# Residual product of a hybrid diffusion backbone cut into four 64x64 blocks, with half of each residual row stored in the other partitions

## Chip, core and metric

The kernel is one program on one core of one Trainium2 chip. The metric is the device time of one launch in microseconds (us); smaller is better. TensorE (PE) multiplies, VectorE (DVE), ScalarE (ACT) and GpSimd (POOL) work elementwise, SyncE (SP) issues most of the loads and stores. PSUM is the memory into which TensorE writes; a bank of it is 512 f32 columns wide on 128 partitions.

## Reference

The reference runs two layers over 1024 latent tokens of 1024 channels. Layer 0 has windowed attention beside a gated linear attention, layer 1 a short gated convolution. Both layers end with a mixture of experts, whose result is added to the residual stream and normalised:

```python
y = hier_moe(tokens, router_wg[l], ..., moe_w1[l], moe_w3[l], moe_w2[l])   # top group, then top-2 of 8 experts
h_lat = post_norm(h_lat, m[5] * y[:B * S].reshape(B, S, D), ln_w[l, 1], ln_b[l, 1])
# post_norm(x, y, w, b) = layer_norm(DEEPNORM_ALPHA * x + y, w, b),  DEEPNORM_ALPHA = (2 * DEPTH) ** 0.25
```

The change concerns the term `DEEPNORM_ALPHA * x` of this last line, in both layers. Everything is f32.

## The kernel before, in words

The 1024 tokens are eight tiles t = 0 to 7 of 128 rows. Each engine has its own instruction stream, written out in order; semaphores tie the streams together.

In `moe(l)` the experts' rows are computed in 21 steps. POOL scatters the rows of a step, already weighted by the gate, to the DRAM tensor `y_rows` (two rows for each token). SP loads the experts' weights piece by piece into slots. When the last piece of a slot has been used, SP fills four of these slots (`ROW_SLOTS`) with the residual rows `h_rows` of two tiles each, and after the last scatter it loads the pairs of expert rows, `pair[t]`, one load for each tile (two half loads for tile 0).

Then comes the stage of this document, the combination. For each tile TensorE makes the sum alpha * x + y in a pair of PSUM banks, (4, 5) for even tiles and (0, 1) for odd ones:

- `residual_part(l, t)` multiplies the residual row tile `row_at[t]` by `alpha_i`, alpha times the identity, once for each 512 columns. It waits for the slot's load and, for t >= 2, for `nrm` of tile t - 2, which frees the banks.
- `combined(l, t)` adds the two expert rows of each token: the tokens 0 to 63 of the tile from `pair[t][:, 0]` and 64 to 127 from `pair[t][:, 1]`, each by a stationary matrix of 128x64, so that two products go to the two halves of the partitions.

TensorE runs the residual products of tiles 0 and 1 right behind `moe(l)`, then `combined` for each tile (with the residual product inside it for t >= 2). In layer 0 the transposes `stream_T(t - 1)` (line 818) follow each `combined`, for the convolution of layer 1; behind the last tile come the products of the convolution (line 1367). Two products `gate_rows` (line 886) stand between the first tiles.

DVE takes the statistics of the sum (1990, 1998), ACT the root (1609), DVE the reciprocal and the offset (2003, 2005), ACT writes the normalised tile (1613) and so sets `nrm`. In layer 1 POOL multiplies the tile by the weight (2661) and DVE adds the bias (2304), two tiles later in its order; SP stores the output. In layer 0 DVE and ACT also copy the transposed tile (1742, 1481), and POOL makes sums of tiles 4 to 6 for the convolution (2636 to 2643), DVE those of tile 7 (2370 to 2377).

Each f32 product is two records in the trace. A semaphore of a slot counts 16 for each load; `filled` works out the count to wait for from `FILLS` and `ROW_LOADS`.

Of the kernel before, what the change touches and what calls it, by code (L numbers as in the profile page):

```python
# [13 lines left out]
P = 128  # L14
# [38 lines left out]
SLOTS = 19  # L53
# [6 lines left out]
SLOT_OF, BEFORE, LAST_IN, FILLS, _held = {}, {}, {}, [0] * SLOTS, []  # L60
# [7 lines left out]
    LAST_IN[_slot] = _piece  # L68
    _held = sorted(_held + [(freed(_piece), _n, _slot, _piece)])
ROW_SLOTS = (9, 11, 14, 15)  # L70
ROW_LOADS = [int(n <= 8 or n in ROW_SLOTS) for n in range(SLOTS)]


def filled(slot, l, turn):

    return 16 * ((FILLS[slot] + ROW_LOADS[slot]) * l + turn + 1)

# [77 lines left out]
def program(nc, T, out):  # L155
# [5 lines left out]
    with ctx:  # L161
        sems = {}

        def S(name):

            if name not in sems:
                sems[name] = ctx.enter_context(nc.semaphore(name))
            return sems[name]

        def sb(name, shape, dt=f32):  # L170
            return ctx.enter_context(nc.sbuf_tensor(name, shape, dt))
# [30 lines left out]
        alpha_i = sb("alpha_i", [P, P])  # L202
# [7 lines left out]
        def bank(b, n=1):  # L210
            return banks[b // 2][:, (b % 2) * 512:(b % 2 + n) * 512]
# [54 lines left out]
        h_dram = [nc.dram_tensor(f"h_rows{l}", [SEQ, D], f32, kind="Internal").ap() for l in range(DEPTH)]  # L266
# [80 lines left out]
        row_at = [blocks[:, 12 + t, :] for t in range(4)] + [hh[:, t] for t in range(4, NT)]  # L347
# [157 lines left out]
        for _s in range(len(SETS)):  # L505
            conv_order += [(_s, n) for n in ((1, 2) if _s >= 2 else ()) + (6, 5, 7, 3, 4)]
        copy_order = [(s, n) for s, (_, m) in enumerate(SETS) for n in ((1, 2, 5) if m == 2 else (1, 2, 5, 4))]
        sum_order = [(s, n) for s, (_, m) in enumerate(SETS) for n in ((11, 22, 12, 21) if m == 2 else (11, 22, 12))]

        def conv_loaded(s):  # L510
# [30 lines left out]
        def _(sp):  # L541
            def load(dst, src, name, **how):
                sp.dma_start(dst, src, **how).then_inc(S(name), 16)  # L543
# [78 lines left out]
            for n, (t0, t1) in enumerate(WOUT_A):  # L622
                sp.wait_ge(S("g_o"), max(t0, t1) + 1)
                for g in range(2):
                    rows = slice(HD * g, HD * g + HD)
# [75 lines left out]
            for l in range(DEPTH):  # L701
# [35 lines left out]
                def last_use(slot):  # L737
                    m, h, q = LAST_IN[slot]
                    if m < 2:
                        sp.wait_ge(S(f"h_mm{l}"), 4 * LAST[q] + 2 * m + h + 1)  # L740
                    else:
                        sp.wait_ge(S(f"y_mm{l}"), LAST[q] + 1)
# [3 lines left out]
                for n, slot in enumerate(ROW_SLOTS):  # L746
                    last_use(slot)
                    dst = blocks[:, 12 + 2 * n:14 + 2 * n, :] if n < 2 else hh[:, 2 * n:2 * n + 2]
                    load(dst, h_dram[l][2 * n * P:2 * (n + 1) * P, :].rearrange("(t p) n -> p t n", p=P), f"w_in_{slot}")
                sp.wait_ge(S("routed"), 8 * l + 8)  # L750
                n_over = sp.value_load(ov[0:1, OVER + 1:OVER + 2], min_val=0, max_val=OVER)
                with sp.If(0 < n_over):
# [25 lines left out]
                for t in range(NT):  # L778
                    rows = y_dram[l][t * 2 * P:(t + 1) * 2 * P, :].rearrange("(h p) n -> p h n", h=2)
# [32 lines left out]
        def _(pe):  # L812
            mm, tp = nc.tensor.matmul, nc.tensor.transpose
# [14 lines left out]
            for k in range(KC):  # L828
                if k % 2 == 0:
                    pe.wait_ge(S(f"ada_in{k // 2}"), 16)  # L830
                for n in range(4):
                    last = mm(bank(0)[32 * n:32 * n + 32, :], cond[:, k, :], ada_first[:, k, n * 512:(n + 1) * 512],
                              start=(k == 0), stop=(k == KC - 1))
# [3 lines left out]
            for k in range(KC):  # L837
                for h in range(2):
                    last = mm(bank(1)[64 * h:64 * h + 64, 4 * k:4 * k + 4], cols(mrow)[:, k, :], cc("pick")[:, 4 * h:4 * h + 4],
                              start=True, stop=True)  # L840
# [562 lines left out]
            def sum_at(t):  # L1403
                return (4, 0)[t % 2]

            def residual_part(l, t):

                slot = ROW_SLOTS[t // 2]
                pe.wait_ge(S(f"w_in_{slot}"), filled(slot, l, FILLS[slot]))
                if t >= 2:  # L1410
                    pe.wait_ge(S("nrm"), NT * (2 * l + 1) + t - 1)
                for n in range(2):
                    mm(bank(sum_at(t) + n), alpha_i[:, :], row_at[t][:, n * 512:(n + 1) * 512], start=True, stop=False,  # L1413
                       skip_group_check=True)

            def combined(l, t):

                if t == 0:
                    pe.wait_ge(S("share_ok"), l + 1)
                if t >= 2:  # L1420
                    residual_part(l, t)
                pe.wait_ge(S(f"w_in_{t}"), filled(t, l, FILLS[t]))
                for n in range(2):
                    if t == 0 and n:
                        pe.wait_ge(S("w_in_8"), filled(8, l, FILLS[8]))
                    for h in range(2):
                        last = mm(bank(sum_at(t) + n)[64 * h:64 * h + 64, :], share[:, t, h, :],  # L1427
                                  pair[t][:, h, n * 512:(n + 1) * 512], start=False, stop=True, skip_group_check=True)
                last.then_inc(S("comb"), 1)
# [13 lines left out]
            for t in range(2):  # L1443
                residual_part(0, t)
# [21 lines left out]
            for t in range(2):  # L1466
                residual_part(1, t)
# [1219 lines left out]
```

## Time and profile before

| | us |
|---|---|
| median of 3 runs | 2289.83 |
| lowest, highest | 2288.42, 2290.57 |
| the profiled execution: its own time | 2290.16 |
| the profiled execution: first to last instruction (span) | 2288.3 |
| TensorE busy | 2166.8 |
| VectorE busy | 808.2 |
| ScalarE busy | 402.3 |
| GpSimd busy | 350.7 |
| mean granted TensorE clock, share of full speed | 0.984 |

The time of the profiled execution is the span and 1.9 us around it. The busy times overlap, and they are sums over the whole program; what a stage of a few microseconds costs is read from the rows of that stage.

### The profile page before, as it was taken

The page shows a single profiled execution, that of the slowest core. Times are in us where ns is not written, and L with a number is a line of the kernel's source. Part 1 is how long each engine was busy: PE and PEld are TensorE (multiplying, and loading weights), DVE is VectorE, ACT ScalarE, POOL GpSimd, SP SyncE. Part 2 cuts the span into 40 slices and gives each one's busy share as a digit, 9 for nine tenths or more (in the row PEclk, how much of TensorE's full clock was granted, in tenths as well). Part 3 has the DMA queues.
Part 4 walks back from the last instruction along what each step waited for, and adds up shares of the span by engine and source line. Part 5 has one row for each costly group of instructions (what it writes and reads, how often), then busy time and mean ns, then how long its engine had stood idle before and what let it go on. Part 6 is the DMA issues. An engine that isn't in the chain of part 4 may idle for free. (4 is left out here: it accounts for less than half of the span.)

```text
span 2288.3 us, 27969 instructions
## 1 busy us (share of the span) xinstructions
PE 2166.8 (95%) x10576; PEld 1047.0 (46%) x10576; DVE 808.2 (35%) x1711; ACT 402.3 (18%) x862; POOL 350.7 (15%) x382
## 2 busy tenths in 40 slices
PE   6999999999999999999997999999998999999996
PEld 3547545777554343434432444444553343334431
DVE  2694213656626311111111633334455111111114
ACT  2301042554211110111110500000111111010112
POOL 0000012222131101100100413221320010201003
PEclk8999999999999999999999999999999999999998
DMA  9892000001436999999998411114337999999997
GB/s 388 332 372 81 1 0 1 2 2 39 145 97 246 371 419 419 419 414 419 409 419 350 175 41 52 37 55 165 141 113 279 417 419 419 408 420 419 411 396 296
DMA packets 135816, 572.50 MB, mean 250 GB/s; under 512 B 25049, under 2 KB 38521, under 8 KB 93690
## 3 DMA queue, kind: packets, MB, share of 16 engines
q1 hardware_dynamic: 123002, 537.04, 59.2%
q0 software_dynamic: 12672, 33.57, 3.8%
q8 instruction: 89, 1.46, 0.3%
q14 instruction: 53, 0.43, 0.1%
HBM read 548.52 MB, written 34.62 MB: 255 GB/s over the span
## 5 line engine op out<-in xcount | busy, mean ns | idle before, releaser
L1291 PE MATMUL bank<-bigA,bigB 128*32 128x512 f32 (+2 forms) x1888 | 478.4, 598 | 13.6 <-DMA bigA<-in_moe_w 8.3
L867 PE MATMUL bank<-bigC,bigB 128*128 128x512 f32 (+3 forms) x768 | 293.7, 538 | 0.0
L1291 PEld LDWEIGHTS bank<-bigA,bigB 128*32 128x32 f32 (+2 forms) x1888 | 157.6, 133 | 237.5 <-issue 229.5
L1315 PE MATMUL bank<-bigA,bigB 128*32 128x512 f32 (+2 forms) x912 | 242.5, 594 | 6.3 <-DVE bigB L2241 3.1
L867 PEld LDWEIGHTS bank<-bigC,bigB 128*128 128x128 f32 x768 | 143.4, 194 | 128.4 <-issue 119.8
L1291 PE MATMUL bank<-bigC,bigB 128*32 128x512 f32 (+2 forms) x560 | 171.4, 593 | 0.0
L1367 PE MATMUL bank<-bigB,bigA 128*128 128x512 f32 x384 | 170.7, 592 | 0.0
L1481 ACT ACTIVATE bigB<-bank,small 128x128 f32<-128x128 f32 x280 | 104.3, 459 | 367.1 <-PE bank L818 367.0
L2565 POOL DMA_INDIRECT y_rows<-bigB,ints x42 | 42.3, 1007 | 810.5 <-DVE bigB L2246 810.5
L2246 DVE TENSOR_TENSOR bigB<-bank,gate 128x512 f32<-128x512 f32 x84 | 54.1, 686 | 236.5 <-PE bank L1315 236.5
L2237 DVE TENSOR_TENSOR bigB<-bigB,bank 128x512 f32<-128x512 f32 x42 | 28.9, 688 | 303.8 <-PE bank L1291 303.8
L1315 PEld LDWEIGHTS bank<-bigA,bigB 128*32 128x32 f32 (+2 forms) x912 | 80.3, 135 | 107.0 <-issue 101.9
L1367 PEld LDWEIGHTS bank<-bigB,bigA 128*128 128x128 f32 x384 | 72.8, 190 | 90.9 <-issue 90.9
L1626 ACT ACTIVATE bigB<-bank 128x512 f32<-128x512 f32 x42 | 25.1, 597 | 498.4 <-PE bank L1291 498.4
L1163 PE MATMUL bank<-bigB,bigA 128*128 128x512 f32 x256 | 112.7, 594 | 0.0
L1367 PE MATMUL bank<-bigA 128*128 128x512 f32 x240 | 109.0, 593 | 2.3 <-issue 1.2
L2241 DVE COPY bigB<-bank 128x256 f32<-128x256 f32 x42 | 17.8, 424 | 243.0 <-PE bank L1299 243.0
L1291 PE MATMUL bank<-misc,bigB 128*32 128x512 f32 (+2 forms) x320 | 101.8, 594 | 1.9 <-DMA bigA<-in_moe_w 1.4
L1315 PE MATMUL bank<-bigC,bigB 128*32 128x512 f32 (+2 forms) x400 | 100.8, 594 | 1.8 <-DMA bigA<-in_moe_w 1.8
L1784 DVE SCALAR_TENSOR_TENSOR lnwb<-bigA,misc,lnwb 128x1024 f32<-128x1024 f32 x70 | 89.9, 1284 | 5.1 <-DMA bigA<-in_ada_w 0.8
L1742 DVE TENSOR_SCALAR bigB<-bank,small 128x128 f32<-128x128 f32 x216 | 73.8, 403 | 25.6 <-PE bank L818 23.2
L1291 PEld LDWEIGHTS bank<-bigC,bigB 128*32 128x32 f32 (+2 forms) x560 | 52.4, 128 | 56.1 <-issue 55.4
(351 smaller groups left out, 2597.0 us busy)
## 6 DMA issues: line engine op xcount, KB each, us to landing
bigA<-in_moe_w SPq DMA_DIRECT2D x250, 1024.0 KB, 24.9
bigC<-in_moe_w SPq DMA_DIRECT2D x80, 1024.0 KB
bigA<-in_ada_w SPq DMA_DIRECT2D x40, 1024.0 KB, 6.8
misc<-in_moe_w SPq DMA_DIRECT2D x36, 1024.0 KB, 24.8
lnwb<-in_moe_w SPq DMA_DIRECT2D x18, 1024.0 KB, 25.9
bigA<-y_rows SPq DMA_DIRECT2D x14, 1024.0 KB, 10.7
bigA<-in_w_in_odd SPq DMA_DIRECT2D x12, 1024.0 KB, 5.2
bigA<-in_ada_w SPq DMA_DIRECT2D x4, 2048.0 KB, 13.6
```

Source lines behind the costliest of these rows:

```text
L867: last = mm(bank(n % 3)[:, 0:w], uT[:, k, t * P:(t + 1) * P], wring[:, g % 2, k, at_:at_ + w], start=(k == 0), stop=(k == KC - 1))
L1163: last = mm(bank(2 * ((t + 1) % 2) + n), zT[:, t, k, :], wout1[:, k, n * 512:(n + 1) * 512], start=(k == 0), stop=(k == KC - 1))
L1291: last = mm(bank(m)[at_:at_ + w, :], xT[:, j, KC // 2 * h + k, at_:at_ + w], w13_at(SLOT_OF[m, h, q][0], k), start=(h == 0 and k == 0), st ...
L1315: last = mm(bank(6 + n)[at_:at_ + w, :], gT[:, 2 * h + k, at_:at_ + w], w2_at(SLOT_OF[2, h, q][0], k)[:, n * 512:(n + 1) * 512], start=(h ...
L1367: last = mm(bank(b[s % 2]), lhs[:, k, :], rhs(k), start=(first and k == 0), stop=(k == 3), skip_group_check=True)
L1481: last = go(dst[k], bank(b + k // 4)[:, (k % 4) * P:(k % 4 + 1) * P], ACT.Identity, bias=shift[:, k:k + 1], scale=scale[:, k:k + 1])
L1626: go(sg, bank(0), ACT.Silu).then_inc(S(f"silu_a{l}"), 1)
L1742: last = v.tensor_scalar(dst[k], bank(b + 1)[:, (k - 4) * P:(k - 3) * P], scale[:, k:k + 1], shift[:, k:k + 1], MUL, ADD)
L1784: V(v.scalar_tensor_tensor(acc[:, r % 2], part, cond[:, k, 0:1], acc[:, r % 2], MUL, ADD))
L2237: v.tensor_tensor(gg, sg, bank(1), MUL).then_inc(S(f"g_d{l}"), 1)
L2246: v.tensor_tensor(yo[:, j, n * 512:(n + 1) * 512], bank(6 + n), gate[:, 1, n * 512:(n + 1) * 512], MUL)\
L2565: pool.indirect_dma_start(out=y_dram[l], out_offset=bass.IndirectOffsetOnAxis(ap=rows, axis=0), in_=yo[:, j], in_offset=None, bounds_check ...
```

## The change

The residual product of a tile is two products of 128 rows by 128 columns before. Since `alpha_i` is diagonal, only two of the four 64x64 blocks of each hold anything. Now these blocks alone are multiplied: four products of 64 rows by 64 columns for each tile, one in each quarter of the array. For this the second 512 columns of each residual row lie in the other half of the partitions: rows 64 to 127 of the tile in partitions 0 to 63 and the other way round. In the products of the first 512 columns (n = 0) block u reads and writes half u; in those of the second (n = 1) it reads half u and writes the other half. The load of two tiles becomes three: one for the first columns, two for the second.

```diff
-ROW_LOADS = [int(n <= 8 or n in ROW_SLOTS) for n in range(SLOTS)]
+ROW_LOADS = [3 * (n in ROW_SLOTS) + (n <= 8) for n in range(SLOTS)]
...
-                    load(dst, h_dram[l][2 * n * P:2 * (n + 1) * P, :].rearrange("(t p) n -> p t n", p=P), f"w_in_{slot}")
+                    rows = h_dram[l][2 * n * P:2 * (n + 1) * P, :].rearrange("(t p) n -> p t n", p=P)
+                    load(dst[:, :, 0:512], rows[:, :, 0:512], f"w_in_{slot}")
+                    for u in range(2):
+                        load(dst[64 * u:64 * u + 64, :, 512:], rows[64 - 64 * u:128 - 64 * u, :, 512:], f"w_in_{slot}")
...
-                pe.wait_ge(S(f"w_in_{slot}"), filled(slot, l, FILLS[slot]))
+                pe.wait_ge(S(f"w_in_{slot}"), filled(slot, l, FILLS[slot] + ROW_LOADS[slot] - 1))
...
                 for n in range(2):
-                    mm(bank(sum_at(t) + n), alpha_i[:, :], row_at[t][:, n * 512:(n + 1) * 512], start=True, stop=False,
-                       skip_group_check=True)
+                    for u in range(2):
+                        rows, to = slice(64 * u, 64 * u + 64), 64 * (u ^ n)
+                        mm(bank(sum_at(t) + n)[to:to + 64, :], alpha_i[rows, 64 * u:64 * u + 64], row_at[t][rows, n * 512:(n + 1) * 512],
+                           start=True, stop=False, skip_group_check=True)
```

On TensorE, in the combination of layer 0, tiles 2 and 3 (818 the transposes of the tile before, 1413 the residual product, 1427 the product with the expert rows), the kernel before has:

```order
L818 MATMUL bank<-misc,bigC 128x128 x8
L1413 MATMUL bank<-bigA,alpha_i 128x512 x2
L1427 MATMUL bank<-bigA,bigB 64x512 x4
L818 MATMUL bank<-misc,bigC 128x128 x8
L1413 MATMUL bank<-bigA,alpha_i 128x512 x2
L1427 MATMUL bank<-bigA,bigB 64x512 x4
```

And the changed kernel, whose lines are numbered three to five higher:

```order
L821 MATMUL bank<-misc,bigC 128x128 x8
L1418 MATMUL bank<-bigA,alpha_i 64x512 x4
L1432 MATMUL bank<-bigA,bigB 64x512 x4
L821 MATMUL bank<-misc,bigC 128x128 x8
L1418 MATMUL bank<-bigA,alpha_i 64x512 x4
L1432 MATMUL bank<-bigA,bigB 64x512 x4
```

Nothing changes its place; two products of the residual become four smaller ones.

On SP, behind the last expert weights of a layer (`ln_w` and `ln_b` are the parameters of the norm, `h_rows` the residual rows), before:

```order
L543 DMA bigA<-in_moe_w 128x2x1024
L543 DMA lnwb<-in_ln_w 128x1024
L543 DMA lnwb<-in_ln_b 128x1024
L543 DMA bigA<-h_rows 128x2x1024 x2
L543 DMA bigC<-h_rows 128x2x1024 x2
```

And after:

```order
L543 DMA lnwb<-in_ln_w 128x1024
L543 DMA lnwb<-in_ln_b 128x1024
L543 DMA bigA<-h_rows 128x2x512
L543 DMA bigA<-h_rows 64x2x512 x2
L543 DMA bigA<-h_rows 128x2x512
L543 DMA bigA<-h_rows 64x2x512 x2
L543 DMA bigC<-h_rows 128x2x512
L543 DMA bigC<-h_rows 64x2x512 x2
L543 DMA bigC<-h_rows 128x2x512
L543 DMA bigC<-h_rows 64x2x512 x2
```

Four loads become twelve, of the same bytes, in runs of 2048 bytes where they were of 4096.

## Rows read from the trace of the kernel before

**Rows 1.** The page, its first line.

```profile
span 2288.3 us, 27969 instructions
```

**Rows 2.** Chain that ended last, layer 1, behind the last scatter: start us, us, what.

```profile
2235.80 7.66 DMA y_rows<-bigB,ints
2243.48 4.09 DMA bigA<-y_rows
```

**Rows 3.** Layer 0: timeline (start, us, operation [idle before]); last, a group (busy, mean ns).

```profile
1270.34 1.16 PE L818 MATMUL bank<-misc,bigC 128*128 128x128 f32 x8
1271.34 1.88 PE L1413 MATMUL bank<-bigA,alpha_i 128*128 128x512 f32 x4
1273.15 1.94 PE L1427 MATMUL bank<-bigA,bigB 128*64 128x512 f32 x8
1275.02 1.16 PE L818 MATMUL bank<-misc,bigC 128*128 128x128 f32 x8
...
1284.49 1.30 DVE L1990 BATCH_NORM_STATS2 small<-bank 128x6 f32<-128x512 f32 x2 [1.07 <-PE bank L1427]
...
L1413 PE MATMUL bank<-bigC,alpha_i 128*128 128x512 f32 x16 | 7.5, 593 | 0.0
```

**Rows 4.** Timeline of TensorE in the attention of layer 0.

```profile
438.93 2.05 PE L1065 MATMUL bank<-bigA,bigC 128*128 128x128 f32 x16
440.91 1.10 PE L1097 MATMUL bank<-bigB,bigC 64*64 64x128 f32 x32
441.94 0.77 PE L970 MATMUL bank<-misc,bigB 128*128 128x128 f32 x5
```

**Rows 5.** Timeline of SP and TensorE, start of the combination of layer 0.

```profile
1237.40 1.55 SPq L543 DMA_DIRECT2D bigC<-h_rows  x2
...
1255.43 7.88 SPq L543 DMA_DIRECT2D bigA<-y_rows  x9
```

**Rows 6.** Timeline of TensorE, the same place.

```profile
1259.64 1.08 PE L1427 MATMUL bank<-bigA,bigB 128*64 128x512 f32 x4 [0.59 <-DMA bigA<-y_rows]
```

**Rows 7.** Timeline of the combination of layer 1.

```profile
2255.07 2.34 POOL L2661 TENSOR_TENSOR bigC<-bigC,lnwb 128x1024 f32<-128x1024 f32 x1 [18.29 <-ACT bigC L1613]
...
2256.17 1.26 DVE L2005 SCALAR_TENSOR_TENSOR small<-small 128x1 f32<-128x1 f32 x1
...
2258.75 2.34 POOL L2661 TENSOR_TENSOR bigC<-bigC,lnwb 128x1024 f32<-128x1024 f32 x1 [1.33 <-ACT bigC L1613]
...
2258.94 1.30 DVE L1990 BATCH_NORM_STATS2 small<-bank 128x6 f32<-128x512 f32 x2 [1.51 <-PE bank L1427]
...
2261.11 0.16 DVE L2005 SCALAR_TENSOR_TENSOR small<-small 128x1 f32<-128x1 f32 x1
...
2262.72 1.30 DVE L1990 BATCH_NORM_STATS2 small<-bank 128x6 f32<-128x512 f32 x2 [0.31 <-PE bank L1427]
...
2264.54 1.94 PE L1427 MATMUL bank<-bigA,bigB 128*64 128x512 f32 x8
...
2266.43 1.96 PE L1413 MATMUL bank<-bigC,alpha_i 128*128 128x512 f32 x4
...
2268.32 1.94 PE L1427 MATMUL bank<-bigA,bigB 128*64 128x512 f32 x8
```

**Rows 8.** Timeline, layer 0, where the combination hands over to the convolution.

```profile
1300.90 1.26 POOL L2636 TENSOR_TENSOR bigA<-bigB 128x512 f32<-128x512 f32 x1 [0.24 <-POOL misc L2643]
...
1309.01 1.48 DVE L2377 TENSOR_TENSOR misc<-bigB,bigA 128x256 f32<-128x256 f32 x1
...
1310.60 3.70 PE L1367 MATMUL bank<-bigA 128*128 128x512 f32 x8 [1.10 <-DVEq L2379]
```

**Rows 9.** Stretches: us, then busy us (instructions) by engine, PEclk, DMA share, GB/s.

```profile
1258.00:1260.00 2.00, 1.41 (x5) 0.42 (x5) 0.00 (x0) 0.91 (x2) 0.00 (x0) 1.00 1.03 381
1261.00:1264.00 3.00, 3.00 (x10) 0.95 (x12) 1.60 (x4) 1.69 (x3) 0.00 (x0) 1.00 1.03 415
1255.00:1257.00 2.00, 2.00 (x5) 0.95 (x4) 0.00 (x0) 0.00 (x0) 0.00 (x0) 0.75 0.13 37
```

## Prediction

> **What bounds the kernel now.** The change touches one stage, the combination behind the experts, once in each layer. So I read no shares of the whole but three views of that stage. The page gives the span, 2288.3 us [rows 1]; the execution's own time was 2290.16, so 1.9 lie around it, and the median shown, 2289.83, is 0.3 below it.
>
> The chain of waits comes first. It shows how the stage begins: the last scatter takes 7.66 us and the first load of expert rows 4.09 [rows 2]. Nothing of TensorE is on the chain there. In layer 0 SP has issued the residual loads by 1238.95 and issues the expert rows at 1255.43 [rows 5]; the first product with expert rows starts at 1259.64, behind 0.59 us of waiting for its load, with the first two residual products in front of it [rows 6]. So the residual products of tiles 0 and 1 are hidden, in both layers, and those of tiles 2 to 7 are what the change can pay for.
>
> The timeline of one tile comes second. In layer 0 a tile takes 4.68 us of TensorE without a gap: 1.00 for the transposes, 1.81 for the residual product, 1.87 for the expert rows (starts at 1270.34, 1271.34, 1273.15 and 1275.02); DVE waits 1.07 us for it in each tile [rows 3]. TensorE is the bound. In layer 1 the tile is two products, 1.89 and 1.89 us (2264.54, 2266.43, 2268.32), 3.78 in all, and DVE waits only 0.31 [rows 7]: two engines are near each other, and a third matters, below.
>
> The third view is what follows. Behind layer 0 the convolution is long TensorE work, then router and experts of layer 1, all started by this chain; I take it that what is won at its start is kept. Behind layer 1 only the norm of the last tile and the stores follow.
>
> **The product itself.** The trace before has blocks of this very shape. In the attention 32 records of 64x64 blocks with 128 columns start at 440.91, and the next work at 441.94: 1.03 us [rows 4]. The eight full 128x128 records of the same width take 1.00 [rows 3]. So four blocks go in the time of one record. For 512 columns the four records of a residual product are busy 1.88 us, of which the last is 0.59 [rows 3]; the three starts before it are 0.43 apart. Four blocks of two records each are two such steps. The expert product, which changes the cut of the array at both ends as the new one will, costs 1.87 for four steps, so 0.15 beyond them. The new product is 2 x 0.43 + 0.15 = 1.01.
>
> The cut of the array now changes in layer 0 where it did not, between transposes and residual product. A record of 128 columns is a quarter of 0.43, 0.107. Sixteen of them between two such changes take 440.91 - 438.93 = 1.98 [rows 4], 0.27 more than their steps, so 0.13 a change; the eight transposes behind one change take 1.00, 0.14 more. I take 0.1, since part of it may already stand in the 0.15. So the tile of layer 0 saves 1.81 - 1.01 - 0.10 = 0.70, six tiles **4.2 us**. In layer 1 a cut changes there already: 1.89 - 0.86 = 1.03.
>
> One thing differs from those rows. There the upper and lower rows of the array write different banks; here both write the same bank, in different halves of its partitions. Each half of the partitions still gets two banks from two row halves, as in the attention, so I expect no conflict. This is my main uncertainty and a rival below.
>
> **What layer 0 keeps.** The new tile needs 3.98 us. DVE's own work is 4.68 - 1.07 = 3.61, so TensorE stays the bound. At the hand-over three things meet: the DVE sums of tile 7 end at 1310.49, the convolution goes on at 1310.60 after waiting 1.10 us for them, and POOL has started its tile 6 at 1300.90 right behind tile 5 [rows 8]. POOL works back to back, 5.7 us a tile, and starts early by less than TensorE does (its tile 4 waits for the fifth tile of the chain, four savings, 2.8). So POOL's last tile lies further into DVE's sums. There the two take turns (next part), and walking through the turns I get the DVE sums 4.0 us earlier, not 4.2. TensorE's 1.10 us of waiting covers the rest. Layer 0 gives **-4.0**; without any of this -4.2, with no cover at all -3.0.
>
> **What layer 1 keeps.** By TensorE alone a tile would fall to 1.03 + 1.89 = 2.92, by DVE to 3.78 - 0.31 = 3.47. But see POOL. DVE's offset instruction, 0.16 us at 2261.11, took 1.26 at 2256.17 and so ended at 2257.43; POOL's product ran from 2255.07 to 2257.41 [rows 7]. I read that DVE's two-input operation from SBUF waits until POOL's ends. Then there is a loop: POOL's product ends, DVE's offset, ACT's write, POOL's next product. It is in the rows: POOL starts at 2255.07 and again at 2258.75, 3.68 us [rows 7]. The tile can't fall below 3.68 while POOL multiplies in it. The page "GPSIMD Engine Reference" of the Trainium skill (1. Specifications) says the same, that GpSimd's SBUF interfaces are shared with VectorE and contended by instructions with two SBUF inputs.
>
> Step by step: the statistics of tile 2 come 0.86 earlier than 2258.94. The offset would then run at 2260.25, while POOL's product (2258.75 + 2.34) ends at 2261.09; it ends at 2261.11, not at 2261.27: 0.16 won of 0.86. Each of the five tiles behind wins 3.78 - 3.68 = 0.10. Layer 1 gives 0.16 + 0.5 = **-0.7**. If POOL were no obstacle, 0.86 and then 0.31 a tile would give -2.4, cut to about -2.2 by tile 3, whose banks are not free before; that is the lower bound, 0 the upper.
>
> **What the loads cost.** Eight more issues take SP 0.5 to 0.8 us each (two took 1.55), some 5 us, up to about 1244; SP's next work is at 1255.43 [rows 5], so this is hidden, and uncovered it would be 5 us. The transfers are another matter. Runs of 2048 bytes (the first expert loads, 1258 to 1260) moved 381 GB/s, those of 4096 (1261 to 1264) 415 [rows 9], 9% more. The residual rows are 4.2 MB, 10.1 us at 415 and 11.0 at 381; eight more completions add little. Some queues still had residual rows when the expert loads were issued: the DMA share is 0.13 from 1255 to 1257 [rows 9], two engines of 16. These lag by up to 0.9 us more, and the first expert load needs all sixteen. Against that, the last scatter alternates with shorter packets and may end sooner. Bounds for each layer -0.5 and +1.0; I take +0.4 in layer 0, where the tail reached into the expert load, and **+0.5** for both.
>
> **Sum.** -4.0 - 0.7 + 0.5 = -4.2 us. The span goes to 2284.1, that execution to 2286.0, the median to 2285.6.
>
> **The rivals.**
>
> *A shared bank is a conflict.* The two blocks of a bank then run one behind the other, and a block of one bank beside a block of the other. The product has four steps, as before, and the change of cut costs 0.1 a tile in layer 0: +0.6, and +0.5 of loads, so +1.1, 2290.9. Against it: the two blocks write different partitions. For it: in [rows 4] the row halves write different banks, and no product before does otherwise. The page "TensorEngine Tiling (Array Packing)" of the Trainium skill (Restrictions and Gotchas, Gotcha 1) says that different row tiles can't access one PSUM bank at the same time, which would be this case. Chance 0.10.
>
> *The blocks run one behind the other altogether (slower).* Place: the residual product of tiles 2 to 7. Four blocks of two steps are 8 x 0.43 + 0.15 = 3.6 us instead of 1.81: +1.8 a tile, over 12 tiles +21; with three of four apart, 6 steps, +0.9 a tile and +11. Say 2300 to 2311. It decides from 4.5 steps on. For it only that no row shows one bank; against it [rows 4]. Chance 0.05.
>
> *POOL is no obstacle in layer 1.* The 1.26 us row is a single one, and DVE might have waited for something else. Then layer 1 gives -2.2 and the sum is -5.7: 2284.1. Chance 0.15.
>
> *The expert loads come later.* If the tail of the residual rows delays each first expert load by 1.0 to 1.5 us, the sum is -4.7 + 2.5 = -2.2: 2287.6. For it the tail [rows 9], against it that in layer 1 there are 7.66 us of scatter in which it drains [rows 2]. Chance 0.15. The opposite, scatters that end sooner by 0.5 a layer, gives -5.7 as well, chance 0.10.
>
> *The forecast*, -3.2 to -5.2: chance 0.45.
>
> **How the numbers follow.** 2285.6 is the forecast's. The range leaves out the serial cases and the best corner: 2283.2 to 2290.2. A measurement tells from no change about 0.2%, 4.6 us, that is 2285.2, close to the forecast; so the forecast's chance is split, 0.16 of it faster. With POOL or the scatter in its favour 0.25 more: faster 0.41. Slower by over 0.2% only with serial blocks or a cause I haven't seen: 0.09. The same: 0.50.
>
> **What would show it.** The four blocks' records should start together, and the residual product should take 1.0 us in place of 1.81, both layers. Layer 0: a tile of 4.0 us; DVE idle before the statistics about 0.4. Layer 1: POOL's products 3.7 us apart, DVE's offset ending with POOL's product in tile after tile, and TensorE waiting in each tile, for the norm or at the end, for the first time. The first product with expert rows, from the issue of its load, 4.1 us as before or up to a microsecond more. The stretch from there to the convolution's 1310.60 should be 4.0 shorter. I am wrong if the blocks of one bank start apart, if DVE's offset stays at 0.16 us while POOL multiplies, or if a later stage (the expert weights of layer 1 come at the pace of DMA) doesn't start earlier with TensorE.

## The result and the profile after

The changed kernel takes 2297.59 us (median of 6 runs, 2294.34 to 2299.26), the kernel before 2289.76 in the runs beside it (6 runs, 2288.42 to 2290.59). The ratio is 1.0033, 95% interval 1.0023 to 1.0044: slower by 0.3%. The forecast was 2285.6 with a range to 2290.2. The profiled execution has a span of 2295.6 us, 7.3 more than [rows 1].

The product did what was forecast. The timeline of TensorE in layer 0 (start, us, operation, idle before it), for [rows 3]:

```profile
1264.01 1.08 PE L1432 MATMUL bank<-bigA,bigB 128*64 128x512 f32 x4 [2.15 <-DMA bigA<-y_rows]
...
1270.05 1.16 PE L821 MATMUL bank<-misc,bigC 128*128 128x128 f32 x8
1271.14 1.09 PE L1418 MATMUL bank<-bigA,alpha_i 64*64 64x512 f32 x8
1272.16 1.94 PE L1432 MATMUL bank<-bigA,bigB 128*64 128x512 f32 x8
...
1276.14 1.94 PE L1432 MATMUL bank<-bigA,bigB 128*64 128x512 f32 x8
```

The residual product takes 1.02 us (1271.14 to 1272.16) for 1.81, and a tile 3.98 (1272.16 to 1276.14) for 4.68. But the first expert product starts at 1264.01, not 1259.64 as in [rows 6], after waiting 2.15 us for its load. In layer 0 the gain is used up before the stage has begun. SP's timeline, for [rows 5]: twelve issues of rows for four, and the expert rows are issued at 1257.57 for 1255.43.

```profile
1235.77 4.74 SPq L543 DMA_DIRECT2D bigA<-h_rows  x6
1240.55 7.14 SPq L543 DMA_DIRECT2D bigC<-h_rows  x6
1257.57 7.28 SPq L543 DMA_DIRECT2D bigA<-y_rows  x8
```

The chain of waits in layer 1, for [rows 2], shows where the time goes: the last scatter takes 10.96 us for 7.66, and the first load of expert rows 7.58 for 4.09. Together that is 6.8 us.

```profile
2237.02 10.96 DMA y_rows<-bigB,ints
2248.00 7.58 DMA bigA<-y_rows
```

Why, the stretches show (us, busy us of PE, PEld, DVE, ACT, POOL, then PEclk, DMA share, GB/s). First the kernel after, while residual rows are coming, in layer 0 and in layer 1:

```profile
1246.00:1253.00 7.00, 1.96 (x2) 0.28 (x3) 0.09 (x1) 0.00 (x0) 0.99 (x1) 0.72 1.07 227
2235.00:2243.00 8.00, 2.32 (x12) 0.80 (x16) 1.22 (x2) 0.00 (x0) 0.98 (x1) 0.75 1.07 220
```

Then the kernel before, in two stretches that stand neither in [rows 9] nor in the prediction. The first is in layer 0's attention, where its own loads of w_out write 64 partitions each; the second is the residual rows.

```profile
522.50:525.00 2.50, 2.03 (x19) 1.24 (x15) 2.47 (x18) 0.49 (x1) 0.37 (x2) 1.00 1.04 261
1246.00:1251.00 5.00, 1.70 (x2) 0.63 (x3) 0.74 (x2) 0.00 (x0) 0.99 (x1) 0.82 1.03 414
```

In all four the DMA engines are busy all the time, yet they move 220 to 261 GB/s where loads that write one half of the partitions are under way, and 414 where all loads write all of them. The share says only that packets are under way; the rate has to be read beside it.

Layer 1, for [rows 7], is as forecast. DVE's offset L2010 (2268.25 and 2272.35) ends with POOL's product (2266.77 + 2.35 and 2270.45 + 2.35), the products start 3.68 us apart, and TensorE waits in each tile for ACT:

```profile
2266.77 2.35 POOL L2666 TENSOR_TENSOR bigC<-bigC,lnwb 128x1024 f32<-128x1024 f32 x1 [1.33 <-ACT bigC L1618]
...
2268.25 0.88 DVE L2010 SCALAR_TENSOR_TENSOR small<-small 128x1 f32<-128x1 f32 x1
...
2270.45 2.35 POOL L2666 TENSOR_TENSOR bigC<-bigC,lnwb 128x1024 f32<-128x1024 f32 x1 [1.33 <-ACT bigC L1618]
2270.52 1.09 PE L1418 MATMUL bank<-bigC,alpha_i 64*64 64x512 f32 x8 [0.73 <-ACT bigC L1618]
...
2272.35 0.47 DVE L2010 SCALAR_TENSOR_TENSOR small<-small 128x1 f32<-128x1 f32 x1
```

The account of the 7.3 us, from the starts of the same work in both traces:

| stretch | before | after | difference |
|---|---|---|---|
| to the first expert product, layer 0 | 1259.64 | 1264.01 | +4.4 |
| from there to the convolution behind its wait (1310.60, 1311.39) | 50.96 | 47.38 | -3.6 |
| from there to SP's first residual load of layer 1 (2224.66, 2225.93) | 914.06 | 914.54 | +0.5 |
| from there to the first expert product, layer 1 (2247.71, 2255.71) | 23.05 | 29.78 | +6.7 |
| from there to the end of the span | 40.59 | 39.89 | -0.7 |

The kernel after issues its first residual load of layer 0 0.6 us ahead of the kernel before (1235.77 and 1236.41), where the two still do the same work. Counted from that issue, as in layer 1, the first expert product of layer 0 comes 5.0 us later (28.24 for 23.23). Up to that issue the kernels of this study differ by as much as 5 us in their profiled executions (1233.5 to 1238.5), though all but shifted_one_input do the same work there. So below, stretches from the first residual issue are compared rather than spans.

The clock is no part of the account. TensorE's granted clock is at its lower level (0.50 of full speed, 1.2 GHz) around the wait for the expert rows of layer 1, from 2246 to 2252 before and from 2240 to 2258 after. But the work behind the wait takes the same time: from the first expert product to POOL's first product 7.36 us before (2247.71 to 2255.07) and 7.37 after (2255.71 to 2263.08).

### The profile page after: what moved, and what is told of

The parts are those of the page before. It is cut to its first block and busy times, and to the rows that moved or that the text cites. A ratio compares the mean times of both kernels' runs of the same rounds, so it can differ in the third digit from the quotient of the medians.

```text
span 2295.6 us, 28113 instructions
## 1 busy us (share of the span) xinstructions
PE 2160.9 (94%) x10640; PEld 1041.1 (45%) x10640; DVE 809.9 (35%) x1711; ACT 402.4 (18%) x862; POOL 351.1 (15%) x382
```

## The experiments

The theory after the result, **PORTS**: a transfer that writes only partitions 0 to 63, or only 64 to 127, runs at about half the rate. The rivals: **RUNS**, the cost is in the shorter pieces (2048 bytes for 4096) and the larger number of transfers; **TURNED**, it is in reading rows in swapped order, or in the blocks.

**1 to 4, on one chip.** Before's product with three loads for one, rows not turned:

```diff
+ load(dst[:, :, 0:512], rows[:, :, 0:512], ...)
+ for u in range(2):
+     load(dst[64 * u:64 * u + 64, :, 512:], rows[64 * u:64 * u + 64, :, 512:], ...)
```

> The product as before (two full products a tile); only the loads are cut as in the change, three for one, but not turned: each 64 partitions get their own rows. Theory PORTS (a transfer that writes only one half of the partitions moves about half as fast, 210 to 227 GB/s in the changed kernel where 415 are moved otherwise): the residual rows take 5 us longer in each layer, the scatter and the expert rows come later, +12 us, about 2302, which is the change's +7.8 plus the 4.7 that its product gives. Theory RUNS (2048-byte runs and more transfers cost this): the same +12. Theory TURNED (reading the rows of the other half costs it): within 1 us of before.

Measured: 2300.40 us, ratio 1.0047 (1.0035 to 1.0059), 10 us above before, where 12 was expected. TURNED falls: neither a swapped row nor a block is in this kernel.

The same number of loads, bytes and pieces, but each of the two writes every other partition:

```diff
-     load(dst[64 * u:64 * u + 64, :, 512:], rows[64 * u:64 * u + 64, :, 512:], ...)
+     load(dst[u::2, :, 512:], rows[u::2, :, 512:], ...)
```

> As the run with loads by half partitions, the same number of transfers, bytes and run lengths, but the second columns go to every other partition (even ones, then odd ones) instead of the lower and the upper 64. PORTS: both halves of the partitions are written at once, so the rate stays near 380 to 415 GB/s and the time is +0 to +2 us, 2290 to 2292. RUNS: +12 us, as with half partitions.

Measured: 2290.32 us for 2290.37, ratio 1.0 (0.9991 to 1.0009). RUNS falls, and PORTS stands: which partitions a load writes makes the 10 us. The stretch with residual rows in layer 0, in the same columns as above, moves 398 GB/s in pieces of 2048 bytes:

```profile
1245.00:1250.00 5.00, 1.12 (x2) 0.49 (x3) 0.70 (x2) 0.00 (x0) 0.99 (x1) 0.86 1.05 398
```

The page "SBUF — State Buffer" of the Trainium skill (Door 1: The DMA port swizzle) states this rule: partitions 0 to 63 reach the 8 even of 16 ports, 64 to 127 the 8 odd ones, so 64 partitions get no more bandwidth than 32. The runs agree, with 215 to 261 GB/s for 386 to 415; they show rates and not the ports themselves, and none loads 32 partitions.

The third takes the four blocks with before's loads:

```diff
+ for u in range(2):
+     rows, to = slice(64 * u, 64 * u + 64), 64 * (u ^ n)
+     mm(bank(sum_at(t) + n)[to:to + 64, :], alpha_i[rows, 64 * u:64 * u + 64], ...)
```

> The four 64x64 blocks of the change with the loads of before, so that the second columns of a tile are not turned and come out with the two halves of its rows exchanged; work and waits on all engines are those of the change but for the loads. My sum without the loads: -4.0 in layer 0, -0.7 in layer 1, -4.7 in all, 2285.1. If the blocks cost more than I think elsewhere, less than that; if they were no gain, 2289.8.

Measured: 2524.78 us, ratio 1.1024. The rows' second column half isn't turned here, so it is added to rows 64 away, and the router of layer 1 sees other values. The groups of TensorE between 2150 and 2460 us (busy us, mean ns, idle before) show the consequence: the experts' overflow loop runs (L1349, L1358, its weights loaded on demand), of which the trace of before has no record.

```profile
L1349 PE MATMUL bank<-bigA,bigB 128*128 128x512 f32 x192 | 97.0, 669 | 84.7 <-DMA bigA<-in_moe_w 84.7
L1358 PE MATMUL bank<-bigA,bigB 128*128 128x512 f32 x80 | 35.7, 599 | 6.1 <-ACT bigB L1632 6.1
```

So its time compares with nothing. Only layer 0's combination can be read, which lies ahead of that router: its first expert product starts at 1258.41 and the last ends at 1288.39, 29.98 us, where before takes 34.15 (1259.64 to 1293.79). The blocks alone win 4.2 us there.

The fourth is the change with the loads into partitions 64 to 127 issued on ACT's queue, behind ACT's work on the experts, to have both halves written at once:

```diff
+ for n, slot in enumerate(ROW_SLOTS):
+     act.dma_start(dst[64:128, :, 512:], rows[0:64, :, 512:]).then_inc(S(f"w_in_{slot}"), 16)
```

> The change, with the loads of the upper 64 partitions issued by ScalarE behind its last work of the experts, so that lower and upper half come from two queues and can be written at once. PORTS: most of the loss goes, the expert rows start within 1 us of before, -2 to -4.5 us, 2285.3 to 2287.8. RUNS: as the change, +8 us or more.

Measured: 2296.72 us, ratio 1.0026 (1.0015 to 1.0037); PORTS as I had put it expected 2285.3 to 2287.8 and missed. Four stretches of it, layer 0 above, layer 1 below:

```profile
1241.00:1246.00 5.00, 4.42 (x14) 1.24 (x10) 0.55 (x1) 0.00 (x0) 0.00 (x0) 0.71 1.06 325
1247.00:1253.00 6.00, 1.76 (x2) 0.19 (x3) 0.00 (x0) 0.00 (x0) 0.99 (x1) 0.81 1.08 214
2228.00:2233.00 5.00, 2.94 (x16) 1.09 (x14) 0.00 (x0) 0.24 (x1) 0.00 (x0) 1.00 0.98 315
2234.00:2240.00 6.00, 0.29 (x2) 0.00 (x0) 1.29 (x2) 0.00 (x0) 0.98 (x1) 0.76 1.06 269
```

This is no more than one queue moves. The change, whose loads all go through SP's queue, has in the first and the third of these stretches:

```profile
1241.00:1246.00 5.00, 3.65 (x16) 1.26 (x16) 1.20 (x2) 0.00 (x0) 0.00 (x0) 1.00 1.03 324
2228.00:2233.00 5.00, 4.17 (x21) 1.34 (x19) 0.00 (x0) 0.00 (x0) 0.18 (x1) 1.00 0.91 312
```

Such an early stretch also holds loads into all 128 partitions, in both kernels. Behind it the rate of the two-queue kernel is 214 to 269. From the first residual issue of SP to the first expert product it takes 29.9 us in layer 0 (1233.48 to 1263.38) and 29.0 in layer 1 (2224.11 to 2253.10), the change 28.2 and 29.8. So the second queue gives back nothing in layer 0 and 0.8 us in layer 1. The profiled span, 2293.0, is 2.6 under the change's, but 2.3 of this stand already ahead of the first residual issue. Against the kernel before, this one costs 6.4 us and the change 7.8, with intervals that overlap. Writing the two halves from two queues did not help here.

**5 to 8, on one chip.** The way out, if PORTS holds: the second column half of row r lies 64 row places further on. Then one load of all 128 partitions that begins 64 rows early turns the rows by itself; only the first and the last 64 rows go alone (two loads of 128 KB), the last into a spare place. The semaphore counts and one more wait that this needs are not shown.

```diff
+ if n == 0:
+     load(dst[64:128, 0, 512:], h_dram[l][0:64, 512:], ...)
+     load(dst[:, 1, 512:], h_dram[l][64:192, 512:], ...)
+ else:
+     late = h_dram[l][2 * n * P - 64:2 * (n + 1) * P - 64, :].rearrange("(t p) n -> p t n", p=P)
+     load(dst[:, :, 512:], late[:, :, 512:], ...)
+ load(normw[0:64, :], h_dram[l][SEQ - 64:SEQ, 512:], "w_in_15")
...
-     mm(..., row_at[t][rows, n * 512:(n + 1) * 512], ...)
+     mm(..., row_at[t + n * (1 - u)][rows, n * 512:(n + 1) * 512], ...)
```

> The change's four blocks with the same values, but no transfer has to write 64 partitions only (but for two of 128 KB): the second column half of row r goes to the row place 64 further on, so that one load of all 128 partitions starts 64 rows early, and the 64 rows that it is shifted past the last tile get a spare place. Theory PORTS (a transfer into one half of the partitions runs at half the rate, and this alone made the change slow): the rows land as before, the last h_rows load within 0.7 us of before's, layer 0's combination keeps its gain of 4.2 us (30.0 us from the first expert product to the last, as in blocks_alone) and layer 1's its 1.3: span 2282.8 + up to 1.5, time 2283.5 to 2286.5, so 3 to 6 us under before. Rival TURNED (a load whose rows do not stand at their own partition, or the product of the blocks from two places, costs time itself): the loads still land 3 to 8 us late, time 2291 or more. Rival GIVEN BACK (the 4.2 us of layer 0 are lost again in the convolution behind it): layer 0's stage is short, but the offset to before at the first convolution product of layer 0 is under 1 us and the time within 2 us of before.

Measured: 2286.48 us for 2289.36, ratio 0.9989 (0.998 to 0.9998), span 2284.2, within PORTS' 2283.5 to 2286.5. The chain of waits in layer 1, then a stretch of residual rows in layer 0:

```profile
2232.21 7.67 DMA y_rows<-bigB,ints
2239.90 4.25 DMA bigA<-y_rows
```

```profile
1246.00:1251.00 5.00, 1.07 (x2) 0.19 (x3) 0.89 (x2) 0.00 (x0) 0.98 (x1) 0.92 1.04 386
```

The scatter and the load are back at 7.67 and 4.25 us [rows 2]. Layer 0's combination takes 29.92 us (1260.01 to 1289.93). Of this 3.6 are still there at SP's first residual load of layer 1 (2221.07 for 2224.66), and 4.1 at the end of the span: the convolution does not give it back.

Next, before's loads as two halves of whole rows, so that all the bytes go into one half at a time, but in pieces of 4096:

```diff
+ for u in range(2):
+     load(dst[64 * u:64 * u + 64], rows[64 * u:64 * u + 64], ...)
```

> The kernel before, with each of its four loads of residual rows cut into one for partitions 0 to 63 and one for 64 to 127, whole rows of 4096 bytes. Theory PORTS: all 4.2 MB now go at some 220 GB/s for 415, so the last h_rows load lands 7 to 10 us later than before in each layer, the first expert product as much, and the time is 2303 to 2312 (twice the 5 us a layer that half of the bytes cost). Rival PACKETS (the half loads were slow only because their packets had 2048 bytes): packets have 4096 bytes as before, time 2289 to 2292.

Measured: 2305.77 us, ratio 1.0075 (1.0059 to 1.009), within PORTS' range. The rate, once it is level, in layer 0 and in layer 1:

```profile
1246.00:1253.00 7.00, 0.92 (x1) 0.50 (x2) 0.37 (x1) 0.00 (x0) 0.98 (x1) 0.70 1.03 229
2244.00:2252.00 8.00, 4.28 (x5) 1.85 (x6) 0.66 (x2) 0.00 (x0) 0.98 (x1) 0.59 1.02 227
```

The last two of this chip look at what paces layer 1. One makes POOL's product with ln_w of 8 columns for 1024, so that the last layer's scale is left out:

```diff
- pool.tensor_tensor(hh[:, t], hh[:, t], lnw, MUL)
+ pool.tensor_tensor(hh[:, t, 0:8], hh[:, t, 0:8], lnw[:, 0:8], MUL)
```

> The kernel shifted, where POOL's product of the normalised rows with ln_w in layer 1 (seven tiles, 2.35 us each) is made of 8 columns for 1024, so the last layer's scale is left out. In the kernel after, layer 1's tiles come 3.68 us apart: ACT's normalisation 1.20, then POOL's product 2.35, and DVE's nm (L2010) ends with POOL's product each time, and ACT's next normalisation starts on it. Theory LOCK (DVE's instruction with two inputs in SBUF stands while POOL's product runs): without it the tiles come 3.0 to 3.4 us apart, paced by PE (2.96) or DVE (some 3.2), and the combination of layer 1 ends 2 to 4.5 us sooner than in shifted. Rival PE BOUND (layer 1 is paced by something else of the tile): 3.68 stays, and the time stays within 1 us of shifted.

Measured: 2284.36 us, ratio to before 0.998 (0.9971 to 0.9989), 2.1 under shifted. Its timeline shows DVE's offset at 0.16 us, and TensorE's residual products 3.37 us apart (2267.56 and 2270.93) for 3.68:

```profile
2267.56 1.09 PE L1425 MATMUL bank<-bigC,alpha_i 64*64 64x512 f32 x8 [0.41 <-ACT bigC L1625]
...
2269.39 0.16 DVE L2017 SCALAR_TENSOR_TENSOR small<-small 128x1 f32<-128x1 f32 x1
...
2270.93 0.65 PE L1425 MATMUL bank<-bigC,alpha_i 64*64 64x512 f32 x2 [0.41 <-ACT bigC L1625]
```

So POOL's product paces layer 1, and PE BOUND falls. Whether it does so through DVE's offset, this run does not tell, since POOL's own time is gone from the loop as well.

The other keeps POOL's product and every value, and gives DVE's offset one tensor input for two:

```diff
- v.scalar_tensor_tensor(nm[:, j:j + 1], mv[:, j, 0:1], -1.0, rs[:, t:t + 1], MUL, MUL)
+ v.tensor_scalar(nm[:, j:j + 1], mv[:, j, 0:1], rs[:, t:t + 1], -1.0, MUL, MUL)
```

> The kernel shifted, where DVE's nm = -mean * rs (128x1) is made by an instruction with one tensor input and rs as its scalar operand, for one with two tensor inputs. Same values. Theory LOCK, second part (only an instruction with two inputs in SBUF waits for POOL; DVE's reciprocal of the same size, with one, starts and ends inside POOL's product): nm takes 0.1 to 0.2 us for 0.47 to 0.88 and ACT's normalisation starts before POOL's product ends. DVE's addition of ln_b (two inputs in SBUF, 1.21) still takes turns with POOL's product (2.35), so the tiles of layer 1 come 3.3 to 3.6 us apart for 3.68, and the time is 0.5 to 2.5 us under shifted. Rival ANY (every DVE instruction of this kind waits for POOL whatever its inputs, and the reciprocal only fell beside it): nm still ends with POOL's product, time as shifted within 0.7.

Measured: 2283.98 us, ratio to before 0.9976 (0.9966 to 0.9987), 2.5 under shifted: the fastest kernel of this study. In the timeline POOL's product runs from 2267.75 to 2270.10; the offset starts at 2269.83 inside it, takes 0.21 us, and ACT's normalisation starts at 2270.08 on it. The next POOL product comes at 2271.36, 3.61 us behind; the one before started at 2264.32, 3.43 ahead. LOCK's second part holds, and ANY falls.

```profile
2267.75 2.35 POOL L2673 TENSOR_TENSOR bigC<-bigC,lnwb 128x1024 f32<-128x1024 f32 x1 [1.07 <-ACT bigC L1625]
...
2269.83 0.21 DVE L2017 TENSOR_SCALAR small<-small 128x1 f32<-128x1 f32 x1
...
2270.08 1.20 ACT L1625 ACTIVATE bigC<-bank,small 128x1024 f32<-128x1024 f32 x1 [0.48 <-DVE small L2017]
...
2271.36 2.34 POOL L2673 TENSOR_TENSOR bigC<-bigC,lnwb 128x1024 f32<-128x1024 f32 x1 [1.26 <-ACT bigC L1625]
```

From the first expert product of layer 1 to the end of the span it takes 38.44 us (2243.16 to 2281.6), shifted 39.92 and shifted_no_scale 37.37. So 1.5 of the 2.5 us are seen in that stage, in one profiled execution of each. Another 1.0 stands ahead of layer 0's first residual load (1235.53 for 1236.56), within what executions differ by there; no run shows whether the edit has a part in it. The steps of 3.43 and 3.61 us alternate, and with them DVE's addition of `ln_b`, which has two inputs in SBUF: it takes 1.22 us, and 1.41 where it starts earlier in POOL's product (2266.35, POOL's ends at 2266.67). That it waits there for POOL fits these rows; no run isolates it.

**9 and 10, one execution each on one chip** (before: 2291.18). Half the bytes in half loads had cost 10 us, all of them 16: is a load into 64 partitions slower with short pieces, or are full loads dragged along between half loads? In the first kernel the four loads of the left columns come ahead of the eight into 64 partitions:

```diff
+ for turned in range(2):
+     for n, slot in enumerate(ROW_SLOTS):
...
+         if turned:
...
+         else:
```

> The kernel before with the three loads for one of loads_half_partitions (2048-byte rows, rows at their own partition), but in another order on SP's queue: first the four loads of the left columns (all 128 partitions), then the eight into 64 partitions. Open is how the two kinds share the time: in loads_half_partitions, where they alternate, both together ran at 217 GB/s, and whole rows in halves (loads_row_halves) at 219 to 255. Theory DRAGGED (a full load between half loads in the queue is slowed by them): by itself the full part runs at 395 to 415 GB/s, then the half part at 215 to 255; the rows land 1 to 3 us sooner than in loads_half_partitions, span 2294 to 2298 for 2299.5. Rival SMALL PACKETS (full loads keep their rate, and half loads with 2048-byte packets run at some 150 GB/s): the half part shows 140 to 170 GB/s, and the span stays within 1.5 us of 2299.5.

Measured: 2298.76 us, span 2296.9. The two parts stand apart in its stretches:

```profile
1242.00:1247.00 5.00, 3.34 (x16) 1.04 (x12) 1.29 (x2) 0.00 (x0) 0.00 (x0) 1.00 1.05 393
1247.00:1253.00 6.00, 0.00 (x0) 0.00 (x0) 0.00 (x0) 0.00 (x0) 0.99 (x1) 0.69 1.07 215
```

393 GB/s for full loads and 215 for half loads, both in pieces of 2048 bytes. But the first expert product of layer 0 comes 29.5 us behind the first residual issue (1265.84 and 1236.33), in loads_half_partitions 28.7 (1264.57 and 1235.92): the order saved nothing there, and 1.3 us in layer 1 (27.2 for 28.5). The rates and the span are DRAGGED's; of the 1 to 3 us that it gave for the rows, only layer 1 shows any.

> The kernel before with each of the four loads of residual rows cut in four: partitions 0 to 63 and 64 to 127, each in its left and its right columns, so that all 4.2 MB go in loads of 64 partitions with 2048-byte packets (loads_row_halves: the same with 4096). Theory DRAGGED: the rate is that of loads_row_halves, 215 to 255 GB/s, first expert product of layer 0 at 1265 to 1267.5, span 2302 to 2305. Rival SMALL PACKETS: some 150 GB/s, the first expert product 6 us or more later than in loads_row_halves in each layer, span 2312 or more.

```diff
+ for u in range(2):
+     for c in range(2):
+         load(dst[64 * u:64 * u + 64, :, 512 * c:512 * c + 512], rows[64 * u:64 * u + 64, :, 512 * c:512 * c + 512], ...)
```

Measured: 2314.62 us, span 2312.5.

```profile
1249.00:1256.00 7.00, 1.37 (x2) 0.84 (x3) 0.63 (x2) 0.00 (x0) 0.99 (x1) 0.68 1.07 227
2248.00:2256.00 8.00, 1.65 (x2) 0.84 (x3) 1.21 (x2) 0.00 (x0) 0.98 (x1) 0.73 1.07 224
```

Neither theory holds whole: the rate of 224 to 227 refutes 150, but the span is the rival's. The rates of loads_row_halves, 227 to 229, are 1 to 2% higher, and 6% above the 215 of loads_columns_first: the length of the pieces, 2048 or 4096 bytes, matters little to half loads. 4.2 MB take 10.1 us at before's 414 GB/s and 18.5 at 227, 8.4 us a layer more. From the first residual issue to the first expert product the two kernels show:

| | before | loads_row_halves | loads_quarters |
|---|---|---|---|
| layer 0 | 23.2 | 31.0 (+7.8) | 32.4 (+9.2) |
| layer 1 | 23.1 | 31.3 (+8.2) | 33.4 (+10.3) |

The spans of the two, 2303.0 and 2312.5, are 9.5 us apart. Only 3.5 of this lie in these two rows, and another 3.5 stand ahead of the first residual issue (1234.99 and 1238.53), where nothing is changed. What the sixteen loads cost beyond the eight stays open; SP issues them in 15.3 us in layer 0 for 5.5.

## Why the prediction was wrong

**The step that failed is "What the loads cost".** It bounded each layer by -0.5 and +1.0 us and took +0.5 for both. Measured: +4.4 in layer 0 (+5.0 from the first residual issue) and +6.7 in layer 1, +11.1. The step priced the length of the pieces (381 for 415 GB/s, [rows 9]) and left out where they go: eight of the twelve loads write 64 partitions. The length by itself costs less than priced: 2048-byte pieces move 393 to 398 GB/s when they go to all or to every other partition. At 215 GB/s for 393, half of 4.2 MB takes 9.8 us for 5.3, an estimate of 4.5 a layer, near layer 0's loss. In layer 1 all of the 6.7 us are in two transfers of the chain, the scatter +3.3 and the first expert load +3.5, so [rows 2] gave no cover: the residual rows still moved at 220 GB/s in the "7.66 us of scatter in which it drains" (2235 to 2243; the scatter starts at 2237.02), and the scatter itself took longer beside them, 10.96 us, and 10.31 in loads_half_partitions, for 7.34 in loads_every_other and 7.67 in shifted. Why the change loses 1.7 us more in layer 1 than in layer 0 stays open; loads_half_partitions loses 5.4 in both. The rival "the expert loads come later" had the place, but priced a tail, 1.0 to 1.5 us, not a rate. Shown by the pair of loads_half_partitions (+10.0) and loads_every_other (0.0), and by shifted, where the loss goes and the gain stays.

**The product** was right: 1.02 us measured, 1.01 forecast, a tile of 3.98, and all eight records in one group of 1.09 us. Two row halves write one bank, in different partitions, without a delay; the "shared bank" and the "one behind the other" rivals fall. The rule of the page "TensorEngine Tiling (Array Packing)" of the Trainium skill (Restrictions and Gotchas, Gotcha 1), which the prediction weighed, does not hold in this case: it would give four steps, as before, where two were measured.

**What layer 0 keeps** was 4.0 by my walk through the turns, and is 3.6 at the convolution in the change (3.85 in shifted, 47.11 from 1260.01 to 1307.12). TensorE waits 1.45 us there, for POOL, not for DVE as in [rows 8]. The line of the kernel after:

```profile
1311.39 1.10 PE L1370 MATMUL bank<-bigA 128*128 128x512 f32 x2 [1.45 <-POOL bigA L2631]
```

**What layer 1 keeps**: forecast -0.7, measured -0.70, of which 0.58 lie between POOL's first and seventh product (22.11 us, 2263.08 to 2285.19, for 22.69, 2255.07 to 2277.76). The loop through POOL's product was read rightly, and shifted_one_input shows its link: with one tensor input DVE's offset no longer waits. "POOL is no obstacle" falls.

**The issues on SP** are twelve for four and hidden, as forecast. They take 11.9 us for 2.5, so the eight more cost 9.4 us where some 5 were priced, and the last is over at 1247.69 (1240.55 + 7.14; about 1244 was forecast), but SP's next work starts only at 1257.57, behind the last scatter.

With the loads at the forecast cost the sum would about have held: shifted keeps product and pace, pays for two loads of 128 KB, and stands at 2286.48 us, 2.9 under before (by the interval of the ratio 0.5 to 4.6), where -4.2 was forecast.

## What to carry to other kernels

Before a tile is laid out so that an engine finds its rows in the other half of the partitions, ask which partitions each transfer writes: into one half of 64 it ran here at 215 to 229 GB/s for some 400, and the DMA share stayed full. A layout that turns rows can be had from full loads, as in shifted, by shifting the whole tensor by 64 rows and giving the last 64 a spare place. And a transfer behind others in the queues has no cover of its own: price it with the rate of what stands ahead of it.

## What the runs showed of the hardware beyond that

- Four 64x64 blocks whose row halves write one bank run together: 1.02 us for eight records of 512 columns.
- Two queues that write opposite halves move no more than one: 315 to 325 GB/s for 312 to 324 where full loads are mixed in, 214 to 269 for 220 to 227 behind that.
- Half loads in pieces of 2048 bytes move 215 to 227 GB/s, in pieces of 4096 bytes 227 to 229: the length matters little beside the partitions.
- Every other partition, 64 in all, is loaded at the rate of full loads: 398 GB/s.
- A DVE instruction on 128x1 with two tensor inputs in SBUF lasted 0.47 to 1.75 us while POOL multiplied, to the end of POOL's product, for 0.16 without it; one with one tensor input took 0.21 inside it. The page "SBUF — State Buffer" of the Trainium skill (Who interferes with whom) has this as an exclusive lock, for two SBUF inputs against a GpSimd instruction that reads SBUF.
- A kernel that alters values ahead of a router can change how much work follows: blocks_alone took 234 us more, with the overflow loop of the experts running.
